# First down projection of a two-block float32 forward pass moved to Strassen's scheme

## The reference, cut to what matters

```python
def conv_ffn(h, w_up, w_conv, b_conv, w_down):
    g, v = jnp.split(h @ w_up, 2, axis=-1)
    g = depthwise_conv_seq(g, w_conv, b_conv)
    return (jax.nn.silu(g) * v) @ w_down          # (512, 2816) @ (2816, 1024)

# end of the first block; gt2 is the sixth part of silu(c) @ w_mod + b_mod
h_lat = h_lat + gt2 * conv_ffn(modulate(h_lat, g_norm_ffn, sh2, sc2), w_up, w_conv, b_conv, w_down)
x = rms_norm(h_lat, g_final)
# second block: opens with rmsnorm(x, g_mix) @ w_in, ends with
x = x + (jax.nn.silu(h2 @ w_ff_gate) * (h2 @ w_ff_up)) @ w_ff_down
return rmsnorm(x, g_final)
```

## Time and profile before

| | us |
|---|---|
| median of 3 runs (lowest to highest) | 1535.33 (1535.27 to 1536.08) |
| the profiled execution, and its span from first to last instruction | 1533.96, 1532.2 |
| TensorE busy, of the span | 1502.9 (98%) |
| first down projection, TensorE, 332.42 to 452.24 | 119.8 |
| second down projection, TensorE, 1397.54 to 1520.40 | 122.9 |

### The profile page before, as it was taken

How to read it: one execution, slowest core, us unless ns; L and a number is a source line. 1 busy time by engine, 2 the same in 40 slices (tenths; PEclk the granted TensorE clock), 3 DMA queues, 4 the chain that set the end, 5 groups by cost and what they waited for, 6 DMA issues and landing times.

```text
span 1532.2 us, 26411 instructions
## 1 busy us (share of the span) xinstructions
PE 1502.9 (98%) x9175; PEld 1349.8 (88%) x9175; DVE 1007.5 (66%) x1551; ACT 602.2 (39%) x1079; POOL 1011.5 (66%) x801
## 2 busy tenths in 40 slices
PE   7999999999999999999999999999999999999897
PEld 6998999998887899988888888888888999999797
DVE  7877787863428477786254565556457787877854
ACT  6543566640113455612032122222335665554442
POOL 4735877766666777766566576476467687776674
PEclk9999999999999999999999999999999999999998
DMA  9942333344232333432322232232232333333232
GB/s 371 404 150 75 104 98 97 109 156 158 98 107 86 97 97 111 123 95 84 95 73 92 80 91 81 77 96 84 65 95 83 110 110 104 102 103 90 86 112 68
DMA packets 235076, 172.89 MB, mean 113 GB/s; under 512 B 5248, under 2 KB 214528, under 8 KB 235008
## 3 DMA queue, kind: packets, MB, share of 16 engines
q1 hardware_dynamic: 235008, 171.98, 35.9%
HBM read 169.86 MB, written 2.10 MB: 112 GB/s over the span
## 4 chain that ended last, share of the span: by engine, by line
PE 58%; DVE 5%; issue 2%; POOL 2%; ACT 1%; DMA 0%; DVEq 0%; POOLq 0%; ACTq 0%
PE ps L1060 19%; PE ps L1064 19%; PE ps L1063 19%; POOL tmp L914 1%; POOL w_lo L932 0%; DVE wide_lo L3039 0%; POOL tmp L923 0%; POOL rope_r L932 0%; DMA raw<-in_w_ff_up 0%; DVE ps L3025 0%; DVE ps L3026 0%; DVE ps L3027 0%; DVE tmp L3024 0%; PE ps L1548 0%; DVE gates_r L3033 0%
## 5 line engine op out<-in xcount | busy, mean ns | idle before, releaser
L1060 PE MATMUL ps<-act_hi,w_hi 128*128 128x256 f32 (+1 forms) x912 | 307.6, 337 | 5.0 <-DVE w_lo L2460 2.0
L900 POOL TENSOR_TENSOR w_lo<-raw,w_hi 128x1024 fp32r<-128x1024 f32 x122 | 305.1, 2501 | 10.2
L1063 PE MATMUL ps<-act_hi,w_lo 128*128 128x256 f32 (+1 forms) x912 | 304.1, 333 | 0.0
L1064 PE MATMUL ps<-act_lo,w_hi 128*128 128x256 f32 (+1 forms) x912 | 304.1, 333 | 0.0
L1060 PE MATMUL ps<-wide_hi,w_hi 128*128 128x512 f32 (+2 forms) x685 | 247.8, 362 | 2.1 <-POOL w_lo L1007 1.1
L1063 PE MATMUL ps<-wide_hi,w_lo 128*128 128x512 f32 (+2 forms) x685 | 247.0, 361 | 0.0
L1064 PE MATMUL ps<-wide_lo,w_hi 128*128 128x512 f32 (+2 forms) x685 | 246.9, 361 | 0.0
L897 POOL TENSOR_TENSOR w_hi<-raw,zero 128x1 fp32r<-128x1 f32 x122 | 31.7, 260 | 281.2 <-PE ps L1060 280.3
L1060 PEld LDWEIGHTS ps<-act_hi,w_hi 128*128 128x128 f32 x912 | 174.1, 191 | 25.4 <-issue 3.2
L1063 PEld LDWEIGHTS ps<-act_hi,w_lo 128*128 128x128 f32 x912 | 174.2, 191 | 17.6 <-issue 1.4
L1064 PEld LDWEIGHTS ps<-act_lo,w_hi 128*128 128x128 f32 x912 | 174.1, 191 | 16.6
(11 more groups left out here) (318 smaller groups left out, 3833.3 us busy)
## 6 DMA issues: line engine op xcount, KB each, us to landing
raw<-in_w_in SPq DMA_DIRECT2D x88, 512.0 KB, 4.0
gates<-in_w_mod_t SPq DMA_DIRECT2D x20, 1024.0 KB, 10.4
raw<-in_w_ffn_up SPq DMA_DIRECT2D x40, 512.0 KB, 3.8
raw<-in_w_ffn_down SPq DMA_DIRECT2D x22, 512.0 KB, 3.6
raw<-in_w_ff_gate SPq DMA_DIRECT2D x22, 512.0 KB, 3.8
raw<-in_w_ff_up SPq DMA_DIRECT2D x22, 512.0 KB, 3.8
raw<-in_w_r_out SPq DMA_DIRECT2D x16, 512.0 KB, 3.4
raw<-in_w_ff_down SPq DMA_DIRECT2D x16, 512.0 KB, 3.7
```

Of the source, the lines that this page charges most:

```text
L900: nc.gpsimd.tensor_tensor(w_lo[:, two, :], raw[:, slot, :], f32(w_hi[:, two, :]), SUB).then_inc(split_done, 1)
L1060: ins = mm(o, w, a, start=start, stop=False)
L1063: mm(o, wl, a, start=False, stop=False)
L1064: return mm(o, w, al, start=False, stop=stop)
```

## The change

The first down projection takes the form of the second. `down_strassen`, `down_act`, `down_dve` and `pool_down` are called for both; for the first the activations' sums lie in `act_hi`, `act_lo` and `gates_r` in the other order. Part 11 is written to banks 6 and 7 and added there by `half_row`. The modulation rows are no longer made at one go: SyncE loads two at a time behind the panels of parts 1, 5, 7 and 9, into two rows of the old `mod_early` tile, and VectorE multiplies each by the kept copy of the silu row, in two instructions of 896 and 128 columns, all operands in SBUF, chained by a semaphore (`late_mod`). Rows 0 and 1 come after the fourth activation sum, rows 2 and 3 in front of the first pair's joins c1 and c2, 4 and 5 with the decay chain before the joins of the second, 6 and 7 before the forms of Strassen unit 5. In both projections the last activation sums (6 and 7) and the first two units' forms are interleaved in another order, and in the second, part 11's first tile does three of its input tiles for the second half of the tokens before the second tile starts.

```diff
-DOWN = FT // 2
+DOWN_STD, DOWN_STRASSEN = 12, 6
@@ SyncE, down_units(f, name), behind the loads of unit u
+                    if f == 0 and u == 1:
+                        sp.wait_ge(product_done, counted(PRODUCTS, pair_of(0, FT - 1), F4))
+                    if f == 0 and u in (1, 5, 7, 9):
+                        for i in range(2):
+                            row = 2 * (1, 5, 7, 9).index(u) + i
+                            if row >= 2:
+                                sp.wait_ge(mod_step, mod_done(5, row - 2))
+                            sp.dma_start(mod_rows[i], w_mod[:, 5, row, :]).then_inc(modw_loaded[i], 16)
-            down_panels(0, "w_ffn_down")
+            down_units(0, "w_ffn_down")
@@ TensorE, down_end (second projection)
-                for s in range(PAIR):
-                    std_tile(f, 11, s, ps[:, 4 + s, halves[0]], halves[0]).then_inc(dn_done[f], 1)
+                std_tile(f, 11, 0, ps[:, 4, halves[0]], halves[0]).then_inc(dn_done[f], 1)
+                std_tile(f, 11, 0, ps[:, 6, halves[1]], halves[1], again=True, blocks=range(3))
+                std_tile(f, 11, 1, ps[:, 5, halves[0]], halves[0]).then_inc(dn_done[f], 1)
                 pe.wait_ge(joined, down_joined(f, 3, "x"))
@@ TensorE, first projection
-            ffn_down(0)
+            down_strassen(0)
+            pe.wait_ge(joined, down_joined(0, 3, "x"))
+            for s in range(PAIR):
+                std_tile(0, 11, s, ps[:, 6 + s, :]).then_inc(dn_done[0], 1)
@@ ScalarE, down_act: order of the first units (both projections)
                 copies(6)
                 sum_copy(unit[0])
-                forms(0, (F1, F6))
+                forms(0, (F1, F6, F7, F5, F2))
                 made(6)
                 late(4)
-                forms(0, (F7, F5, F2))
                 copies(7)
-                forms(0, (F3,))
+                forms(0, (F3, F4))
+                sum_copy(unit[1])
+                forms(1, (F1,))
                 made(7)
                 late(5)
-                form_hi_of(F4, unit[0])
-                sum_copy(unit[1])
+                forms(1, (F6, F7, F5))
                 late(6)
+                forms(1, (F2,))
                 late(7)
-                forms(1)
+                forms(1, (F3,))
@@ ScalarE, down_act: end for the first projection
+                act.wait_ge(t_ready, t_at(f, "late", 7))
+                act.wait_ge(mod_step, mod_done(5, KT - 1))
+                for m in range(4):
+                    square_both(m)
+                form_hi_of(F4, unit[5])
+                act.wait_ge(product_done, counted(PRODUCTS, unit[4], F4))
+                for m in range(3):
+                    gained_hi(1, m, gain_12[:, m:m + 1])
+                down_half_copy(f, 3)
...
@@ VectorE, down_dve (both projections; late_mod and decays in the first only)
                 for k in range(1, 6):
...
+                    if late_mod and k == 3:
+                        late_mod(0)
+                        late_mod(1)
...
                 down_parts(f, 6)
+                lo(F6, 0)
                 down_t_sums(f, 6)
-                lo(F6, 0)
-                down_lo(f, 6)
-                down_late(f, 4)
                 lo(F5, 0)
                 add3(unit[0])
-                down_parts(f, 7)
+                down_lo(f, 6)
+                down_late(f, 4)
                 lo(F3, 0)
+                down_parts(f, 7)
                 down_t_sums(f, 7)
                 add6(unit[1])
                 down_lo(f, 7)
-                down_late(f, 5)
-                down_late(f, 6)
-                down_late(f, 7)
                 lo(F6, 1)
+                down_late(f, 5)
                 lo(F5, 1)
                 add3(unit[1])
+                down_late(f, 6)
+                down_late(f, 7)
                 lo(F3, 1)
...
                 join_parts(1)
                 add3(unit[2])
-                finish(1, 0)
                 lo(F3, 2)
-                finish(1, 1)
+                for s in range(PAIR):
+                    if late_mod:
+                        late_mod(2 + s)
+                    finish(1, s)
...
+                if late_mod:
+                    late_mod(4)
+                    late_mod(5)
+                    decays()
                 join_parts(2)
...
                 lo(F3, 4)
+                if late_mod:
+                    late_mod(6)
+                    late_mod(7)
                 add6(unit[5])
...
+                for m in range(1, 4):
+                    add_squares(m)
+                for m in range(2):
+                    gained_lo(1, m, gain_12[:, m:m + 1])
+                join_parts(3)
...
+            def late_mod(m):
+                w, partial = mod_rows[m % 2], small[:, m // TT, m % TT:m % TT + 1]
+                dve.wait_ge(silu_row_copied, 3)
+                dve.wait_ge(modw_loaded[m % 2], 16 * (len(MOD_ORDER) - 1 + m // 2 + 1))
+                for (sl, kept), start, dst in zip(silu_kept, (mod_bias(5)[:, m:m + 1], partial), (partial, mod[:, 5 * KT + m:5 * KT + m + 1])):
+                    ins = nc.vector.tensor_tensor_reduce(out=w[:, sl], in0=w[:, sl], in1=kept, scale=1.0, scalar=start,
+                                                         op0=MUL, op1=ADD, accum_out=dst)
+                    if dst is partial:
+                        link(ins)
+                ins.then_inc(mod_step, 1)
+            def half_row(m):
+                dve.wait_ge(dn_done[0], m - 3)
+                dve.wait_ge(dn_free[0], m + 1)
+                scaled_row(m, ps[:, m, :]).then_inc(dn_free[0], 1)
```

More of the change, by code:

```diff
@@ L1041, in pool_down, with splits @@
                 std_split(f, 11, 1)
+            def splits(first, last, loads):
+                with pool.Fori(first // RAW, last // RAW) as i:
+                    for u in range(RAW):
+                        split_more(i * RAW + u, i, u, loads)
+                for p in range(last // RAW * RAW, last):
+                    split_more(p, p // RAW, p % RAW, loads)
+            pool_first(pair_of(0, EIGHT))
+            pool_periods(0, FT)
+            pool_down(0)
+            splits(MIX, SEVEN[2] - 2, FNET_LOADS + MIX_LOADS)
+            pool_first(pair_of(2, 0))
+            pool_periods(2, MIXES)
+            splits(HEAD0, SEVEN[1] - 2, FNET_LOADS + LOADS[1])
+            pair0, pair1 = pair_of(1, 0), pair_of(1, 1)
+            last_split(SEVEN[1] - 2, FNET_LOADS + LOADS[1])
+            add5(pair0)
+            add7(pair0)
+            last_split(SEVEN[1] - 1, FNET_LOADS + LOADS[1])
+            form_lo_of(F7, pair0)
+            form_lo_of(F2, pair0)
+            form_lo_of(F5, pair0)
+            form_lo_of(F1, pair0)
+            add5(pair1)
+            add7(pair1)
+            form_lo_of(F4, pair0)
             pool_periods(1, FT)
@@ L1349, in std_tile @@
                 pe.wait_ge(split_done, p + 1)
-                for b in range(n):
+                for b in blocks or range(n):
                     if j == 0:
@@ L1981, in _ @@
+            down_act(0)
             for k in range(2):
@@ L2759, in _, with down_parts @@
[L2759 to L2761 removed]
+            def down_parts(f, k):
+                bank, (a, b) = DOWN_T_BANK[k], down_rows(k)
+                b11, b12, b22 = ps[:, bank, halves[0]], ps[:, bank, halves[1]], ps[:, bank + 1, halves[1]]
+                dve.wait_ge(gained, LOADED + T_SUMMED[3 + f] + k + 1)
+                if k >= 4:
+                    dve.wait_ge(t_ready, t_at(f, "late", k - 4))
+                tt(down_t1(k), b12, f32(wide_lo[:, a, halves[1]]), ADD)
+                tt(b11, b11, f32(wide_lo[:, a, halves[0]]), ADD)
+                link(tt(b22, b22, f32(wide_lo[:, b, halves[1]]), ADD))
@@ new lines, in down_lo, with down_late @@
+            def down_lo(f, k):
+                dve.wait_ge(t_hi_made, LOADED + t_at(f, "lo", k))
+                c = k // QUAD
+                hi, lo = (w[:, k % QUAD, :, :] for w in down_t[f][c])
+                tt(lo, down_sums(k), f32(hi), SUB).then_inc(t_ready, 1)
+            def down_late(f, k):
+                dve.wait_ge(t_hi_made, LOADED + t_at(f, "late", k))
+                hi, lo = (w[:, down_rows(k)[0], halves[1]] for w in (wide_hi, wide_lo))
+                tt(lo, down_t1(k), f32(hi), SUB).then_inc(t_ready, 1)
```

644 lines of the change are left out of this document (291 added, 353 removed).

## The result

The changed kernel takes 1547.14 us (median of 4 runs, 1546.44 to 1547.55) against 1535.30 for the kernel before on the same chip: a ratio of 1.0077, 95% interval 1.0064 to 1.0089, 11.8 us slower. The profiled execution took 1547.54 us, its span is 1545.8.

The account below looks back on a forecast made before the run. TensorE, busy 1502.9 of 1532.2 us, was taken as the bound, with VectorE pacing inside stages. First projection +9.4 and second -3.05 gave +6.35 on the profiled 1533.96: 1540.3, as a median 1541.7, range 1533 to 1550.

Parts of the forecast that it names:

- TensorE's work, -3.5: First projection: 119.8 us of wide matmuls removed, 116.3 added by Strassen's form, 3.5 us saved.
- Start, +8.4: First projection up to unit 2: VectorE late through rows 0 and 1 (5.8 us); +8.4 us, bounds 5.8 and 10.0.
- that rule: Modulation rows: VectorE instructions with two SBUF inputs and GpSimd instructions reading SBUF exclude each other; 25.6 us for eight rows.
- Units 2 to 5, +1.5: First projection's middle: VectorE's forms, rows, decay chain and joins make TensorE wait; +1.5 us, bounds 0 and 4.7.
- End, +3.0: First projection's end: F4 behind ScalarE's squares, then GpSimd's split of part 11 and join x; +3.0 us, bounds 0 and 4.5.
- Clock, nothing: All stretches: granted clock 1.00 in the earlier trace, so no term is one of clock.
- Second projection, -3.05: Second projection: new order of first forms gains 1.95 us, part 11's end gains 1.1 us.
- Loads, nothing: First projection: SyncE's waits for modulation rows stand before panels wanted some 8 us later; no cost.
- rival D: SyncE's queue: a modulation row's wait holds back part 8's panels; 1545.7 us, slower, chance 0.08.
- B: Rival: modulation-row halves meet no GpSimd instruction, middle and end cost nothing; 1534.6 us, no change, chance 0.2.
- C: Rival: order of forms takes all waits from units 0 and 1, gain 4.3 us; 1529.9 us, faster, chance 0.12.
- A: Rival: VectorE late in the first projection, as the terms sum; 1541.7 us, slower, chance 0.6.

Follow-up runs that it names:

- rows of one operand and a column: Changed kernel, each half of a modulation row multiplied by one column instead of the kept row, not summed, bias copied (rows wrong): 1544.20 us.
- plain sums: Changed kernel, each half of a modulation row a tensor_reduce sum over w, no product with the kept row (rows wrong): 1536.71 us.
- everything moved: Changed kernel, nothing left out; rows 4 and 5, decay steps, F4's form, gained rows and joins placed in another order: 1545.18 us.
- the run with the end reordered: Changed kernel, F4 of unit 5 formed before ScalarE's squares, third pair's joins before VectorE's additions and gained rows: 1546.77 us.
- the run without rows: Changed kernel, all eight modulation rows left out and the rest of the first projection in another order: 1536.07 us.

## Why the forecast had the sign and half of the size

I forecast 1541.7 (6.35 us above the profiled execution of before) and measured 1547.14, inside the range of 1533 to 1550. The stage was to take 129 us and took 137.0. That the total stayed in the range is not the merit of each term: the end left its own bound of 4.5 by 4, and the start came out under its forecast.

**TensorE's work, -3.5.** Right: the stage's 137.0 us close with 116.3, to 0.1 us.

**Start, +8.4.** Unit 2 starts 66.2 us into the stage, not 67.85: +6.7, inside the bounds. Of that 5.4 us are waits, where I had named 7 to 10 as the sign, and 1.4 the lower clock. The clock is no cost of its own here. VectorE sets unit 2's start: from unit 0's first matmul to unit 2's it is 24.63 us in the changed kernel, and 24.61 and 24.60 with rows of one operand and a column and with plain sums, where the clock is 1.00 throughout. What TensorE does not lose to the clock there it waits, in unit 1, as this line of the run with plain sums shows and the changed kernel does not:

```profile
384.83 0.39 PE L1066 MATMUL ps<-gates_r,w_hi 128*128 128x256 f32 x1 [1.17 <-DVE w_lo L2449]
```

So the start was put 1.7 us too high: 0.6 of it is rows 0 and 1, which took 5.2 us where I forecast 5.8, 0.35 the order's larger gain (61.4 for 61.75), and 0.8 I can't place. It was the two halves that I had named that stretched (355.16 and 356.04). One reading behind it was wrong, though its number held: the 8-column instruction of the earlier trace rows, which I gave as one with two SBUF operands and as agreeing with that rule, is L2743, a `tensor_scalar` with one SBUF operand and a constant. It showed beforehand that one operand can be enough, and the run with a column was spent on finding that out.

**Units 2 to 5, +1.5.** Mis-sized: 3.9. The stretch that I had summed as 12.0 us, rows 4 and 5 with the decay chain, takes 14.8 (412.71 to 427.50): 7.2 for the rows where I had 5.0, and 7.6 for the chain where I had 7.0. All eight rows take 22.2 us on VectorE, where I had 20.8.

**End, +3.0.** The step that failed: 5.7 us of waits and 2.8 of clock behind them. F4's wait was right (9.0 less 7.2, measured 1.76). For part 11 the sum has only GpSimd's split, 2.9 less 1.44; the join x behind additions and gained rows is named, and has no term. It was the join that released part 11, after 3.98 us of waiting. Two gained rows in front of it took 3.58 us for 1.5, and an addition 1.76 for 0.7. I used the rule of two SBUF operands for the rows, where it was at stake, and not for these instructions, which have two as well.

**Clock, nothing.** The sentence "no term below is one of clock" failed. All five stretches of the earlier trace rows had 1.00, with waits up to 2.03 us. In the changed kernel 4.2 us of slower matmuls stand in its place, of which the 1.4 of unit 0 cost nothing in the end, as said above, and the 2.8 of part 11 have no wait behind them that they could shorten.

**Second projection, -3.05.** Right: -3.3, of which the order 2.2 (forecast 1.95) and part 11 1.1 (forecast 1.1). The waits for F7 and in part 11 are gone.

**Loads, nothing.** Right: no wait in the first projection is released by a load, so rival D did not happen.

Of the rivals, B has the runs against it by the plain sums: free of GpSimd, the rows' kernel comes to 1536.7, near B's 1534.6; with the true rows it is 10.4 us more, and their halves stretch in the trace. C needed unit 2 of the second projection at 60.6 us or earlier, and it came at 61.4. Its price was also put too low: it takes the lower bound of the start and nothing for the middle and the end; with A's terms for these the same gain of 4.3 gives +1.65 and not -5.4. Its idea was good in another place: 2.25 us more did lie in the order of the second projection's joins and late subtractions. What a better order cannot do is take away VectorE's work in the first projection: it moved 5.7 us of waits from F4 and part 11 into the convolution, and everything moved at once gained 0.7 us at the gates.

Where the expected gain of Strassen's form went: 3.5 us off TensorE, against 12 us of VectorE work for the eight rows, which had cost nothing where they stood before, lengthened to 22 by GpSimd, in a stage where VectorE already had the activations' sums, the forms and the joins. With the rows out of the way these alone took the 3.5 back, and 2.4 more.

## What to carry to other kernels

Before moving work onto a half-idle engine, make two sums for the stage it goes to: its durations there, and its durations if each instruction of a kind that a trace shows stretching beside GpSimd waits for one of GpSimd's. Decide by the second (here 25.6 us for the rows, of which 22.2 came), for the old instructions of the stage as well as the moved ones. Before adding up losses of TensorE, ask which of them another engine's lateness would have cost anyway. When a new order moves waits and not the end, stop reordering and take work out. And test an edit that is bundled with a large one by itself: here the small one gained 0.3% alone, and the large one hid it.

## What the runs showed of the hardware that was not expected

TensorE's granted clock fell to its lower level, 1.2 GHz, inside a stage in which it is 89% busy. Every wait of 2.9 us or more in the first projection (2.91 to 5.13 us, in six kernels) was followed within 1.6 us by 11 to 26 matmuls at that level. Shorter waits did it sometimes: 1.89 us in front of part 11 (7 wide matmuls), 1.80 in front of unit 4 in one kernel, and not 1.80 and 1.78 at the same place in two others, nor 2.14 before unit 0. In the convolution there was none behind the four waits of 1.2 to 1.9 us of the run with the end reordered, but 7 wide ones behind those of 1.96, 2.53 and 1.24 with everything moved, and 6 behind the 5.54 of the run without rows. What decides in the short cases is open. The slower matmuls are 1.3 to 2.8 us of TensorE's time behind a wait of 2.9 us or more; they are a loss where TensorE is the engine that the rest waits for (part 11), and none where it would wait for VectorE next (unit 0).

VectorE's `tensor_scalar` from SBUF to SBUF, with a column as well as with a constant, waits for GpSimd like an instruction with two SBUF operands: 8 columns took 1.22 us (the decay chain's L2928 at 424.04 in the changed kernel) where the chain's last four instructions take 0.17 each. `tensor_reduce` over the same columns of the modulation rows did not: 1.07 to 1.08 us for every 896.
